# Token scales from token-major tiles of x, squared on ScalarE and spread through DRAM, instead of two groups of matmuls

## The reference, cut to what matters

```python
h = rmsnorm(x, pre_g)                    # x * rsqrt(mean(x*x) + 1e-6) * g, per token (1024 tokens, 1024 features)
p = h @ w_in                             # 1024 x 3328, columns for q, k, v, gates of two groups of heads
ya = sliding_window_sink_attention(...)  # group A: 8 heads, 2 kv heads
yb = differential_attention(...)         # group B: 4 heads, two softmax maps each, v of 128 columns a head
y = concat(ya * silu(ag), yb * silu(bg)) @ w_out
out = x + rmsnorm(y, post_g)
```

## Time and profile before

| what | value |
|---|---|
| time, median of 3 runs | 520.45 us (519.73 to 521.59) |
| the profiled execution's own time | 522.18 us |
| its span, first to last instruction | 520.4 us |
| granted TensorE clock, mean | 0.995 |
| PE busy | 97% of the span |
| DVE, ACT, POOL busy | 55%, 50%, 22% |
| HBM read and written | 26.88 MB and 4.19 MB |

### The profile page before, as it was taken

The page is one execution under the profiler, slowest core; times in us unless marked ns, Lnnn a source line. Parts: engine busy times, 40 slices in busy tenths (PEclk is TensorE's granted clock), DMA queues, the critical chain, the costliest instruction groups (busy, mean ns, idle before and its releaser), DMA issues.

```text
span 520.4 us, 7482 instructions
## 1 busy us (share of the span) xinstructions
PE 504.6 (97%) x2724; PEld 422.9 (81%) x2724; DVE 286.2 (55%) x672; ACT 259.8 (50%) x622; POOL 116.1 (22%) x143
## 2 busy tenths in 40 slices
PE   8999999999999999999999899999999989999995
PEld 8999987888787878888877677788788868888884
DVE  4959733565656456446465786535673574433332
ACT  7932634555665647556576855533553361321211
POOL 1070513223032022302135235311303440000000
PEclk9999999999999999999999999999999989999999
DMA  8810042110111010111011011011000824332222
GB/s 315 258 46 0 2 120 81 38 43 3 38 43 40 2 40 2 41 41 42 1 40 42 1 42 30 12 42 40 1 0 6 227 93 132 111 121 82 81 88 75
DMA packets 41540, 32.05 MB, mean 62 GB/s; under 512 B 18784, under 2 KB 36128, under 8 KB 41504
## 3 DMA queue, kind: packets, MB, share of 16 engines
q1 hardware_dynamic: 38912, 26.85, 18.3%
q10 hardware_dynamic: 2592, 4.72, 2.5%
HBM read 26.88 MB, written 4.19 MB: 60 GB/s over the span
## 4 chain that ended last, share of the span: by engine, by line
PE 83%; ACT 5%; issue 4%; DVE 3%; DMA 3%; POOL 1%; SPq 0%; DVEq 0%; POOLq 0%; ACTq 0%
PE proj L1234 37%; PE scores L1340 15%; PE scores L1165 8%; PE scores L1255 6%; PE banks L1276 5%; PE banks L1266 3%; PE banks L1321 2%; PE proj L1165 1%; PE banks L1165 1%; PE scores L1301 1%; PE banks L1309 1%; DMA w_raw<-in_w_in 1%; DMA wo_early<-in_w_out 1%; ACT weights L823 1%; ACT k_stack L803 1%
## 5 line engine op out<-in xcount | busy, mean ns | idle before, releaser
L662 POOL TENSOR_TENSOR w_lo<-w_raw,w_hi 128x256 fp32r<-128x256 f32 x84 | 63.0, 778 | 173.3 <-ACT w_hi L748 173.3
L1234 PE MATMUL proj<-hT_hi,w_hi 128*128 128x512 f32 x336 | 89.9, 400 | 1.2 <-DVE k_stack L1015 0.6
L1234 PE MATMUL proj<-hT_hi,w_lo 128*128 128x512 f32 x336 | 89.4, 400 | 0.0
L1234 PE MATMUL proj<-hT_lo,w_hi 128*128 128x512 f32 x336 | 88.5, 400 | 0.0
L1070 DVE CUSTOM_DVE_ANT_0 weights<-scores,dist_b 128x128 f32<-128x128 f32 (+7 forms) x64 | 45.9, 754 | 53.8 <-PE scores L1255 53.7
L1234 PEld LDWEIGHTS proj<-hT_hi,w_hi 128*128 128x128 f32 x336 | 60.5, 188 | 14.4 <-DVE k_stack L1015 1.0
L1234 PEld LDWEIGHTS proj<-hT_hi,w_lo 128*128 128x128 f32 x336 | 60.6, 188 | 13.3 <-issue 1.9
L1234 PEld LDWEIGHTS proj<-hT_lo,w_hi 128*128 128x128 f32 x336 | 60.6, 188 | 11.8 <-issue 0.8
L823 ACT ACTIVATE weights<-weights,small 128x128 f32<-128x128 f32 (+7 forms) x64 | 49.0, 767 | 15.1 <-DVE small L1070 15.1
L833 ACT ACTIVATE weightsT<-banks 128x512 f32<-128x512 f32 (+3 forms) x48 | 23.6, 491 | 56.1 <-PE banks L1266 56.0
L1255 PE MATMUL scores<-k_stack,q_stack 128*128 128x512 f32 (+3 forms) x192 | 41.8, 353 | 0.0
(11 more groups left out here) (129 smaller groups left out, 760.3 us busy)
## 6 DMA issues: line engine op xcount, KB each, us to landing
w_raw<-in_w_in SPq DMA_DIRECT2D x13, 512.0 KB, 4.0
w_raw<-in_w_in SPq DMA_DIRECT2D x16, 256.0 KB, 3.8
x_res<-in_x SPq DMA_DIRECT2D x8, 512.0 KB, 4.5
out<-y_out ACTq DMA_DIRECT2D x16, 256.0 KB, 2.3
x_all<-in_xT SPq DMA_DIRECT2D x7, 512.0 KB, 7.1
wv_raw<-in_w_in SPq DMA_DIRECT2D x8, 160.0 KB, 6.7
wo_early<-in_w_out SPq DMA_DIRECT2D x4, 256.0 KB, 4.3
w_raw<-in_w_out SPq DMA_DIRECT2D x4, 256.0 KB, 6.3
```

Source lines behind the costliest of these rows:

```text
L662: nc.gpsimd.tensor_tensor(w_lo[:, n % SPLIT, k], w_raw[:, n % RAW, k], w_hi[:, n % SPLIT, k].bitcast(F32), ALU.subtract).then_inc(w_lo_rea ...
L1234: last = nc.tensor.matmul(to, w[:, slot, k, :], h[:, k, HALF * half:HALF * half + HALF], start=(p == 0 and k == first), stop=(p == PIECES ...
```

## The change

The scales no longer use PE or `x_all`. SP loads `x` a second time, token tile by token tile (`x_rows`, 128 tokens by 1024 features, 512 KB each) into three buffers. ACT squares each tile with an accumulator, which gives the mean square of its 128 tokens directly. POOL adds the epsilon and takes the root, in two parts of four tiles. SP writes the four columns of a part to DRAM (`write_scales`, 512 elements of 4 bytes) and loads them back spread over all partitions (`load_scales`, 256 KB) into `scale_rows` in SBUF. The first column group of v is stored without a scale and multiplied in place later (`scale_v`). DVE normalises in two halves of 512 tokens. `scale_rows` shares its place with the second buffer of `w_raw`, so w(1) is loaded after the normalisation. `high_weights(1)` moves behind the last `high_again`, `make_lambda()` behind the last low part.

```diff
+            def load_rows(t):
+                if t >= ROWS:
+                    sp.wait_ge(x_squared, t - ROWS + 1)
+                sp.dma_start(x_rows[t % ROWS][:, :], x[0, t * P:(t + 1) * P, :]).then_inc(rows_loaded[t % ROWS], 16)
+            def write_scales(part):
+                tiles = slice(4 * part, 4 * part + 4)
+                sp.wait_ge(x_scaled, part + 1)
+                sp.dma_start(scales[tiles, :].rearrange("t p -> p t"),
+                             x_scale[:, tiles], allow_slow_non_contiguous=True).then_inc(scales_written[part], 16)
+            def load_scales(part):
+                sp.wait_ge(scales_written[part], 16)
+                sp.dma_start(scale_rows[:, HALF * part:HALF * part + HALF],
+                             scales.rearrange("t p -> (t p)")[HALF * part:HALF * part + HALF]
+                             .unsqueeze(0).to_broadcast([P, HALF])).then_inc(scales_loaded[part], 16)
...
             for part in range(KT // 2):
-                if part == 2:
-                    pool.wait_ge(x_meaned, 1)
-                    root(x_scale, x_mean, TILES, x_scaled)
...
+            for part in range(2):
+                tiles = slice(4 * part, 4 * part + 4)
+                pool.wait_ge(x_squared, 4 * part + 4)
+                nc.gpsimd.tensor_scalar(x_mean[:, tiles], x_square[:, tiles], 1.0, EPS, ALU.mult,
+                                        ALU.add).then_inc(x_meaned, 1)
+                pool.wait_ge(x_meaned, part + 1)
+                root(x_scale[:, tiles], x_mean[:, tiles], 4, x_scaled)
...
+            def square_x(t):
+                act.wait_ge(rows_loaded[t % ROWS], 16 * (t // ROWS + 1))
+                if t:
+                    act.wait_ge(x_squared, t)
+                rows = x_rows[t % ROWS]
+                nc.scalar.activation(rows[:, :], rows[:, :], ACT.Square, scale=D_MODEL ** -0.5,
+                                     accum_out=x_square[:, t:t + 1]).then_inc(x_squared, 1)
...
+            def scale_v(t):
+                act.wait_ge(x_scaled, t // 4 + 1)
+                act.wait_ge(v_stored, t + 1)
+                part = v_sb[:, t, 0:VG]
+                nc.scalar.activation(part, part, ACT.Copy, scale=x_scale[:, t:t + 1]).then_inc(v_scaled, 1)
...
             def high_again(t):
                 tokens = slice(P * t, P * t + P)
-                act.wait_ge(x_normed, KT)
+                act.wait_ge(x_normed, KT * (t // 4 + 1))
...
-                if k > 1:
-                    add_squares(k - 1)
-            add_squares(KT - 1)
-            dve.wait_ge(x_summed, 1)
-            nc.vector.tensor_scalar(x_mean, x_sums, 1.0 / D_MODEL, EPS, ALU.mult, ALU.add).then_inc(x_meaned, 1)
-            dve.wait_ge(x_scaled, 1)
-            for t in range(TILES):
-                nc.vector.tensor_scalar(diagonals[:, P * t:P * t + P], ident[:, :], x_scale[:, t:t + 1], None,
-                                        ALU.mult).then_inc(diagonals_made, 1)
             constants()
...
-            pe.wait_ge(squares_added, KT - 1)
-            for t in range(TILES):
-                done = nc.tensor.matmul(x_sums[:, t:t + 1], square_sum[:, P * t:P * t + P], ones[:, 0:1],
-                                        start=True, stop=True)
-            done.then_inc(x_summed, 1)
...
-                    for half in range(2):
-                        cols = slice(HALF * half, HALF * half + HALF)
-                        nc.tensor.matmul(scale_rows[:, cols], ones[:, :], diagonals[:, cols],
-                                         start=True, stop=True).then_inc(scale_spread, 1)
```

101 lines of the change are left out of this document (57 added, 44 removed).

## The result

| | before | changed |
|---|---|---|
| time, median of 4 runs each (lowest to highest) | 520.61 us (519.73 to 521.59) | 535.02 us (534.29 to 536.56) |
| the profiled execution's own time, its span | 522.18, 520.4 us | 535.11, 533.3 us |
| granted TensorE clock, mean | 0.995 | 0.981 |

The ratio is 1.0284, with a 95% interval of 1.0256 to 1.0311: slower, as forecast, by 14.4 us instead of 9.2. The time of 535.02 lies inside the range (525.5 to 536.5), close to its upper end.

A forecast was written before the change was run, and what follows sets the result against it. PE, busy 504.6 of 520.4 us, bounds the kernel. Idle 13.3 us, less 3.43 of removed scale matmuls and 0.57 already idle, supports +9.2: 531.4 against the profiled run, 529.7 as median forecast; range 525.5 to 536.5.

The forecast's parts named there:

- the write: SP's write of the first scales to DRAM, 512 pieces of 4 bytes: 3.4 us, bounds 2.1 and 6.8.
- the small loads: Six loads late in SP's queue, needed by DVE's constants: last issued at 48.8, landing in 4.0 us at 52.8.
- a second half of 31 us: From DVE's first normalisation to unit 1 on PE, through splits, stores and w(2): 31.4 us.
- S: Start of DVE's normalisation of the first half: forecast 56.8, against 44.30 before.
- a slow restart before unit 1: PE at half clock after idling before unit 1: 1.8 us, uncovered there; the clock rival's cost, chance 0.2.
- a late small load: Allowance of 1.6 us in the range's upper end for a small load landing late, at its bound of 5.6.
- The rival of a slow write at 6.8: Write of the scales at its bound of 6.8 us: +3.4 on S, 533.1 us; chance 0.2.
- the first scales: After ACT's square 3 and POOL's multiply and root: first scales ready at 41.5.
- This costs nothing here: PE in v, result 13 needing store 9: tile 7 near 50.0, store 9 at 53.2, result 12 at 53.3; no cost.
- The clock: Rival: slow PE restart costs 1.8 us, covered before unit 0's second half but not before unit 1; 531.5 us, chance 0.2.
- the trace had borne a wait of 2.1 us: PE's clock: a last gap shortened to 2.6 us before unit 1 was called about what the earlier trace had borne.
- After unit 1 PE gives nothing back: PE behind unit 1 is full again, so none of the +9.2 us is recovered.

The follow-up runs named there:

- e1_probe: Kernel before plus five chained transfers on SP's idle queue: 4-, 16- and 64-byte-piece writes and a spread load; 520.64 us, one run.
- e7_probe: Kernel before plus other chained transfers in SP's idle stretch: small pieces spaced or side by side, a 4-byte-piece load; 519.68 us, one run.
- e8_warm: Changed kernel plus unused small identity matmuls on PE before result 13 and both halves of unit 0; 539.55 us.
- e3_sixteen: Changed kernel with scales written as 128 pieces of 16 bytes and read by DVE with a 16-byte step; 534.64 us.
- e4_both: Changed kernel with both w(0) and small loads first and scales in 16-byte pieces read with a step; 524.96 us.
- e2_small_first: Changed kernel with w(0) and the six small loads ahead of the row loads in SP's queue; 531.81 us.
- e6_early16: e5_early with row tiles of every fourth token, 16-byte-piece writes read in order, v's scale columns loaded back, and SP reordered; 514.55 us.
- e5_early: Changed kernel, 4-byte writes kept, with row loads, squares, small loads and first root earlier, writes issued together, both halves normalised in one stretch; 520.5 us.

## Why the prediction was right and wrong

**Direction, place and chain: right.** It said that the write, SP's order and the small loads would hold the first normalisation, that a second half of 31 us would follow and that PE would idle before both halves of unit 0 and before unit 1. The distance was 30.8 instead of 31.4. Tile 3 ended ACT's wait before the fourth square (1.35 us), the small loads ended DVE's idle time, and ACT's last wait before unit 1 was for w(2).

**The write: the step that failed.** I put it at 3.4 us, from v_shift in the earlier trace rows, because both have 512 pieces, and at 6.8 at most. It took 8.9. The analogy went by the number of pieces; e1_probe shows 128 pieces of 4 bytes at 7.1 and 128 pieces of 16 bytes at 1.4, e7_probe that 4-byte pieces are quick when they lie apart. As far as e7_probe tells, the quantity that decides is how many pieces share a small stretch of DRAM, and no row of before has it. Twice the nearest row was no bound; 5.5 us of the 6.5 on S come from here. That the time still lay inside the range is in part luck: the range's upper end was made of a write of 6.8, a slow restart before unit 1 (1.8) and a late small load (1.6); the restart did not come, and an early start and the 2.1 us behind unit 1 helped. The rival of a slow write at 6.8, with its chance of 0.2, was the right one and still 2.1 us too quick.

**The small terms on S.** The slab phase ended at 30.68 instead of the 32.20 before, and tile 3 landed in 4.1 us instead of 4.5; with the hand-overs the first scales were there at 39.05, 2.4 us ahead of the forecast 41.5. 1.5 us of that is luck of the run: the slab phase ends at 30.6 in e8_warm and at 32.6 in e3_sixteen, whose edits act only later, and at 30.6 in e4_both and 32.6 in e2_small_first, which load in the same order. The nine issues behind the write took up to 1.11 us each instead of 0.43 to 0.47 (+1.1), the last landed in 4.86 instead of 4.0 (+0.8), and DVE's constants took 5.46 us instead of 4.04 (+1.4). The last has a neighbour: POOL's low parts of w(0), 59.37 to 63.21, run beside DVE's constants, where before POOL was idle. One of these constants, in the changed kernel first, then in the kernel before:

```profile
61.80 0.82 DVE L997 SCALAR_TENSOR_TENSOR dist_a<-dist_a 128x128 f32<-128x128 f32 x1
```
```profile
43.79 0.28 DVE L951 SCALAR_TENSOR_TENSOR dist_a<-dist_a 128x128 f32<-128x128 f32 x1
```

In e8_warm POOL's low parts ran earlier against DVE, from 60.78 to 63.58. The same instruction, at 64.59, took 0.28 there, and the constants 4.94 in all.

Together: -2.4 + 5.5 + 1.1 + 0.8 + 1.4 = 6.4, against the 6.5 found.

**"This costs nothing here": wrong as a wait, right as a cost.** I had tile 7 landing near 50.0 and PE not held in v. Tile 6 landed at 51.27 and PE waited 6.02 us for store 9. But v does not hold unit 0: that waits 2.20 us more, for ACT's splits, and these for the normalisation. In e3_sixteen the wait inside v is gone, and PE stands 6.67 us before unit 0's first half instead of 2.20. PE is early there, and where it spends that makes no difference.

**The clock: the mechanism right, its place wrong.** The rival said that a slow restart before unit 0's second half is covered and shortens the last gap, and that a slow restart before unit 1 costs. In the changed kernel unit 0's second half did run slowly, the last gap was 1.11 us, and unit 1 started at full clock: no cost. e8_warm turned this round and paid it, and so, in part, did e3_sixteen, whose unit 1 started slowly behind a wait of 2.11 us (3.08 us for eight matmuls). The remark that the trace had borne a wait of 2.1 us was a misreading of the earlier trace rows. The row gives the wait only. The timeline of the kernel before shows what came behind it:

```profile
425.82 3.52 PE L1340 MATMUL scores<-wo_hi,hT_hi 128*128 128x512 f32 x8 [2.10 <-ACT hT_hi L882]
```

and its window of PE (window, busy us and count, granted clock, DMA share, GB/s) shows the clock:

```profile
425.00:430.00 5.00, 4.18 (x11) 0.66 0.00 0
```

**"After unit 1 PE gives nothing back": wrong in the profiled pair.** In the changed kernel the same place, the first product of the output projection, waits 1.29 us and the clock stays up:

```profile
439.88 1.89 PE L1367 MATMUL scores<-wo_hi,hT_hi 128*128 128x512 f32 x7 [1.29 <-ACT hT_hi L935]
```

That is 0.8 us of wait less, and from the first product to the third group of eight 4.2 us (to 444.12) instead of 5.4 (425.82 to 431.18): together 1.9 us, most of the 2.1 by which the span gained on unit 1. The kernel before does not lose this in each run: with the transfers of e1_probe it waited 1.50 us there and restarted at full clock, and its span was 518.8 us.

What the wait hangs on is a race between two engines, and the traces show it. ACT's `hT_hi`, for which PE waits, needs DVE's `out_B`. Beside it POOL makes a low part of the output weights. In the changed kernel POOL starts first, and DVE's instruction takes 2.87 us; in e2_small_first DVE starts first, and the same instruction takes 0.69:

```profile
435.56 2.39 POOL L726 TENSOR_TENSOR wo_lo<-w_raw,wo_hi 128x1024 fp32r<-128x1024 f32 x1 [1.64 <-ACT wo_hi L838]
435.63 2.87 DVE L1072 TENSOR_TENSOR out_B<-gate,out_B 128x512 f32<-128x512 f32 x1
```
```profile
435.03 0.69 DVE L1072 TENSOR_TENSOR out_B<-gate,out_B 128x512 f32<-128x512 f32 x1
435.21 2.77 POOL L726 TENSOR_TENSOR wo_lo<-w_raw,wo_hi 128x1024 fp32r<-128x1024 f32 x1 [1.90 <-ACT wo_hi L838]
```

In five traces POOL starts first; `out_B` then takes 2.17 to 2.87 us, ends 0.54 or 0.55 us after POOL's instruction each time, and PE waits. In the other five DVE starts up to 0.21 us ahead of POOL (in e6_early16 both start within 0.01 us), `out_B` takes 0.69, and PE does not wait. So in these traces a tenth of a microsecond goes with 0.6 to 2.1 us of waiting near the end, far behind what was edited, and the start of unit 1 is the better measure of these edits:

| profiled run | S | unit 1 | `out_B` | wait at the output projection | span |
|---|---|---|---|---|---|
| before | 44.30 | 79.02 | 2.17 | 2.10, slow restart | 520.4 |
| e1_probe | 44.61 | 79.32 | 2.17 | 1.50 | 518.8 |
| e7_probe | 44.21 | 78.56 | 2.18 | 1.20 | 517.9 |
| changed | 63.26 | 94.05 | 2.87 | 1.29 | 533.3 |
| e2_small_first | 56.01 | 93.42 | 0.69 | none | 530.7 |
| e3_sixteen | 58.06 | 95.04 | 0.69 | none | 533.9 |
| e4_both | 45.78 | 83.86 | 2.17 | 0.59 | 522.6 |
| e5_early | 53.02 | 78.16 | 0.69 | none | 515.4 |
| e6_early16 | 42.06 | 75.14 | 0.69 | none | 512.5 |
| e8_warm | 65.10 | 95.92 | 0.69 | none | 534.7 |

Between the medians the loss is 14.4 us. How often either engine starts first in the runs without a trace is not known.

## What to carry to other kernels

Before a transfer is costed by its piece count, look at where its pieces land: 4-byte pieces side by side in DRAM took 7 to 10 us in an idle queue and in a busy one, the same numbers in 16-byte pieces 1.4 in the probe and 1.4 to 4.8 in the kernels. Two loads issued behind or beside the slow write were slow too (11.8 us instead of 5.3, 8.6 instead of 5.0). Choose the layout so that both ends are plain, since a step of 16 bytes on VectorE's side took back all that the write had given. And a chain that replaces work on the busiest engine gains only if it ends before that engine needs it: the same change cost 14.4 us when its squares began at 31 us, nothing when they began at 19 (e5_early, with its other edits), and gained 5.75 with quicker writes as well. And before a gain of 2 us is put down to an edit, see in the traces whether it arises where the edit acts.

## What the runs showed that I had not expected

- Writes of 512 neighbouring 4-byte pieces: 8.1 to 10.0 us in nine transfers of five kernels. 128 such pieces 7.1, at 64 bytes from each other 1.4; 8-byte neighbours 3.1; 16-byte neighbours 1.4 in the probe, 1.4 to 4.8 in the kernels.
- SCALAR_TENSOR_TENSOR of 128x512 with one input read at a step of 16 bytes: 1.05 us, in order 0.67. The edit also writes the other operands in two dimensions; that was not moved alone.
- A DVE instruction that starts while POOL runs a tensor_tensor waits for it: `out_B` takes 0.69 us ahead of POOL's and ends 0.55 us after POOL's end where POOL was first (rows above); the constants' 128x128 took 0.82 us instead of 0.28. No run moved POOL alone; the traces differ by chance.
- A wait's length alone does not tell whether the clock falls. Behind waits of 2.10 us (the kernel before), 2.20 (the changed kernel, before unit 0) and 2.11 (e3_sixteen, before unit 1) the next eight matmuls took 3.52, 3.59 and 3.08 us; behind waits of 2.34 (e5_early) and 2.20 (e8_warm) they took 2.11.

One window of the changed kernel at unit 0's start shows the low level, columns as for e8_warm:

```profile
74.00:76.00 2.00, 2.00 (x6) 1.52 (x6) 2.00 (x4) 0.00 (x0) 0.00 (x0) 0.50 0.00 0
```

The granted clock is 0.50 of full speed, which is 1.2 GHz. The two windows of 2 us ahead of it have 1.00 and 0.75, the one behind it 0.89, with PE busy throughout from 73.16.
